# Front end of a hybrid decoder step: where the chunk row gathers, the second load of input weights and the first low weights are issued

## The reference, cut to what matters

```
xn = rms_norm(x, norm_attn_g)
z  = xn @ w_in                      # every q, k, v, gate and forget column at once
q, k heads = rms_norm per head
o_cmp, o_sel = nsa_cmp_sel(...)     # rows of cache_cmp_k/v in chunks of 16 -> small MLP -> compressed keys
                                    # and values, then attention on those and on the best 16 blocks
o_win = window_attend(...)          # last 512 rows
o_fox = fox_attend(...)             # logits plus sums of log forget gates, old ones from cache_fox_logf
h = x + (sig(ga) * (o_a @ w_o_a) + sig(gb) * (o_fox @ w_o_b)) @ w_out
y = h + (gelu(causal_conv3(rms_norm(h) @ w_up)) * (rms_norm(h) @ w_gate)) @ w_down
```

## Time and profile before

| | us |
|---|---|
| median of 3 runs | 945.47 |
| lowest and highest | 944.38, 947.38 |
| the profiled execution | 945.58 |
| its span, first to last instruction | 943.70 |

### The profile page before, as it was taken

How to read it: one execution, slowest core, us unless ns; L and a number is a source line. 1 busy time by engine, 2 the same in 40 slices (tenths; PEclk the granted TensorE clock), 3 DMA queues, 4 the chain that set the end, 5 groups by cost and what they waited for, 6 DMA issues and landing times. The chain is left out here.

```text
span 943.7 us, 18057 instructions
## 1 busy us (share of the span) xinstructions
PE 866.1 (92%) x7225; PEld 710.1 (75%) x7225; DVE 524.4 (56%) x980; ACT 367.8 (39%) x662; POOL 162.3 (17%) x262
## 2 busy tenths in 40 slices
PE   2999858989999999999999977999979999999996
PEld 1778747878988987665765455998669998989884
DVE  4556648743343567763466534565756565566554
ACT  3246445543334324453224321443344443534330
POOL 0200122210031012323334521000002010110100
PEclk9999969999999899999999989999989999999999
DMA  6434296039234339989999995986044544564412
GB/s 215 135 125 147 86 242 227 3 105 217 91 130 167 152 122 405 337 309 391 408 420 418 395 400 187 293 234 235 9 152 163 177 134 133 181 199 153 133 44 59
DMA packets 90608, 191.89 MB, mean 203 GB/s; under 512 B 7434, under 2 KB 68650, under 8 KB 78154
## 3 DMA queue, kind: packets, MB, share of 16 engines
q0 software_dynamic: 15408, 106.04, 29.3%
q1 hardware_dynamic: 73836, 84.43, 28.9%
q10 hardware_dynamic: 1296, 0.45, 0.2%
HBM read 187.44 MB, written 7.64 MB: 207 GB/s over the span
## 5 line engine op out<-in xcount | busy, mean ns | idle before, releaser
L1581 PEld LDWEIGHTS banks<-consts_base,stream_rows 128*128 128x128 f32 x672 | 73.2, 141 | 31.0 <-issue 27.3
L1828 ACT ACTIVATE keys_turned<-banks 128x512 f32<-128x512 f32 x94 | 55.0, 597 | 100.3 <-PE banks L1581 100.2
L258 PE MATMUL banks<-tokens_turned_high,w_gates_high 128*128 128x288 f32 x288 | 86.1, 299 | 3.5 <-PEq L191 2.3
L1581 PE MATMUL banks<-consts_base,stream_rows 128*128 128x128 f32 x672 | 82.5, 275 | 4.7 <-PEq L191 1.7
L259 PE MATMUL banks<-tokens_turned_low,w_gates_high 128*128 128x288 f32 x288 | 85.0, 295 | 0.0
L1120 PE MATMUL banks<-chunks_turned_high,cmp_w_high 64*128 64x256 f32 (+1 forms) x512 | 78.4, 300 | 5.3 <-DVE cmp_w_low L251 2.7
L260 PE MATMUL banks<-tokens_turned_high,w_gates_low 128*128 128x288 f32 x272 | 81.3, 299 | 0.0
L1120 PE MATMUL banks<-chunks_turned_low,cmp_w_high 64*128 64x256 f32 (+1 forms) x512 | 75.4, 288 | 0.0
L1120 PE MATMUL banks<-chunks_turned_high,cmp_w_low 64*128 64x256 f32 (+1 forms) x512 | 75.2, 287 | 0.0
L1809 DVE COPY keys_turned<-banks 128x512 f32<-128x512 f32 x74 | 50.4, 689 | 29.6 <-PE banks L1581 27.1
L251 DVE TENSOR_TENSOR chunks_turned_low<-banks,chunks_turned_high 128x512 fp32r<-128x512 f32 x64 | 41.1, 683 | 41.6 <-ACT chunks_turned_high L246 41.6
(11 more groups left out here) (446 smaller groups left out, 2114.6 us busy)
## 6 DMA issues: line engine op xcount, KB each, us to landing
w_up_gate<-in_w_up SPq DMA_DIRECT2D x12, 1024.0 KB, 7.4
w_up_gate<-in_w_gate SPq DMA_DIRECT2D x12, 1024.0 KB, 9.8
w_down<-in_w_down SPq DMA_DIRECT2D x12, 1024.0 KB, 5.1
w_in_slot<-in_w_in SPq DMA_DIRECT2D x8, 1424.0 KB, 6.2
w_gates<-in_w_in SPq DMA_DIRECT2D x10, 512.0 KB, 6.6
cmp_w<-in_cmp_w_k SPq DMA_DIRECT2D x4, 512.0 KB, 8.5
cmp_w<-in_cmp_w_v SPq DMA_DIRECT2D x4, 512.0 KB, 12.3
stream_rows<-in_state_win_k SPq DMA_DIRECT2D x8, 256.0 KB, 8.5
```

The lines of the kernel that those rows point to most:

```text
L258: nc.tensor.matmul(out, lh, rh, start=start, stop=False, **kw)
L1581: ins = nc.tensor.transpose(bank(t)[:, q * P:(q + 1) * P], src, ident)
L1828: copy = lambda a, b: nc.scalar.activation(a, b, ACT.Copy)
```

## The change

Three edits, all before the compression stage:

1. The four chunk row gathers leave POOL's list in `stage_project`, with POOL's three waits in front of them. In `stage_prompt` they stand behind POOL's copies; the m-th waits for `qk` to reach m + 1. The eight gathers of log forget values follow, and the b-th now waits for `qk` to reach b + 5.
2. The load of the second part of `w_in` leaves `stage_tokens` and becomes SP's first instruction in `stage_project`.
3. The low part of round 0 is made in two halves of four row groups each. The first half raises the new semaphore `first_low`, the second raises `low`. PE's wait before `tokens(0, 0)` is for `first_low`; a wait for `low` stands in the middle of it, before its fifth row group.

```diff
@@ stage_tokens, block.sync
-            for u in range(2):
-                load_w_in(c, sp, w, w_loaded, u, ORDER[u] * ZC)
+            load_w_in(c, sp, w, w_loaded, 0, ORDER[0] * ZC)
@@ stage_project
-        low = c.sem("w_in_low_ready")
+        low, first_low = c.sem("w_in_low_ready"), c.sem("w_in_first_low_ready")
@@ stage_project, block.sync
         def _(sp):
+            load_w_in(c, sp, w, w_loaded, 1, at(1))
             for n, g in enumerate(("k_norm_sel_g", "k_norm_win_g", "k_norm_b_g")):
@@ stage_project, block.gpsimd
             ins.then_inc(chunks.w2z, 1)
-            pool.wait_ge(low, NZC)
-            pool.wait_ge(z_sums, 3 * NZC - 2)
-            pool.wait_ge(heads_turned, number["QA", 2])
-            for m in range(NB):
-                chunks.gather(m)
@@ stage_project, block.tensor, tokens(n, t)
                 for k in range(KD):
+                    if (n, t, k) == (0, 0, KD // 2):
+                        pe.wait_ge(low, 1)
...
-                pe.wait_ge(low, n + 1)
+                if n == 0:
+                    pe.wait_ge(first_low, 1)
+                else:
+                    pe.wait_ge(low, n + 1)
                 tokens(n, 0)
@@ stage_project, block.vector
-            split(0)
+            dve.wait_ge(high, 1)
+            for half in range(2):
+                k = slice(half * KD // 2, (half + 1) * KD // 2)
+                split_low(nc, wl[0][:, k, :], w[0][:, k, :], wh[0][:, k, :]).then_inc((first_low, low)[half], 1)
@@ stage_prompt, block.gpsimd
             nc.gpsimd.tensor_copy(c.png[:, :, :], z[:, 0:2, O_NG:O_NG + 3 * NH])
+            for m in range(NB):
+                pool.wait_ge(qk, m + 1)
+                chunks.gather(m)
             link = c.chain(pool, "gpsimd")
             for b in range(DB):
-                pool.wait_ge(qk, b + 1)
+                pool.wait_ge(qk, NB + b + 1)
                 nc.gpsimd.indirect_dma_start(past_logf[:, b]...
```

## The result

The changed kernel takes 933.07 us (median of 6 runs, 930.44 to 936.61) against 945.77 us for the kernel before (6 runs, 944.38 to 947.66). The ratio is 0.987, with a 95% interval from 0.9851 to 0.9889. So the prediction was wrong in size: it expected a gain of 8.4 us and 12.7 came. The times of the changed kernel fall into two groups, 930.4 to 930.8 and 935.4 to 936.6, and its profiled execution is the slowest of the upper one: 936.61, with a span of 933.8 (2.8 lie around it, 1.88 before).

The account below looks back on a forecast made before the run. PE was taken as the bound inside project, with a gather-held hole before prompt. Gains of 7.6 + 0.5 + 0.3 = 8.4 us gave 937.1 us, range 933.5 to 940.5.

Parts of the forecast that it names:

- The hole, part 1: End of project: gathers in flight keep PE idle 10.5 us before prompt; moving them leaves about 2.9, gaining 7.6 us.
- The rival that it isn't the gathers': End of project: slow meeting or another transfer makes the hole; only 0.5 us gained, 945.0; 4 in 100.
- The cost of the moved gathers: Prompt stage: four gathers added on POOL delay log rows and sums, but within their cover; cost nothing.
- the bound of 163.6: Prompt stage: latest landing of the log rows, in us; the stage's end is delayed only if they land after 172.5.
- The clock in prompt: Early prompt: a shorter hole may keep PE at full clock; gain 0 to 2.0 us, taken as 0.3.
- the lower bound: Early prompt: no clock gain, 0 us, since PE still has a 2.9 us gap and the clock may fall there.
- Part 2's gain: Tokens stage: the second weight load came wholly after the first and took nothing from it; gain 0, at most 3 us.
- The rival with an earlier first slot: Start of project: first weight slot lands earlier, by up to 3 us, 1.5 in the middle; 935.6 us; 10 in 100.
- Part 2's cost: Project stage: moved load lands at 29.1 to 29.8, third weight part about 35.2, both in time; cost nothing.
- Part 3: Start of project: halving the first low part removes PE's 0.58 us wait; gain 0.34 to 0.58 us, taken as 0.5.
- The later stages: After the edits: a sign; the prediction is wrong if later stages lose what was gained; no size given.
- Part 2's own upper bound of 3: Tokens stage: at most 3 us gained if DMA engines that finish early slow the others through memory.

Follow-up runs that it names:

- e5: Kernel before with two of the four chunk gathers left in the project stage and two moved to prompt; 943.05 us (one run) beside 945.51.
- e6: Kernel before with the four chunk gathers replaced by four plain 1 MB loads of SP behind the same waits; 935.08 us (one run) beside 945.51.
- e2: Kernel before with only the second weight slot's load moved into the project stage; 944.01 us (12 runs), ratio 0.9975.
- e7: Kernel before with the page numbers loaded by SP in the project stage instead of by ACT in tokens; project started at 19.68 us, total time not given.
- e8: Changed kernel with the page numbers loaded by SP in the project stage, behind the gains; 943.5 us (12 runs), ratio 0.998 to the kernel before.
- e10: The changed kernel run again, nothing altered; 935.48 us (6 runs), ratio 0.9879 to the kernel before; its profiled execution is of the lower group.
- e14: Kernel before with only the first low part made in halves, a repeat profile; it and another repeat took 941.25 and 941.33 us.

## Why the prediction was right and where it failed

- **The hole, part 1: right, mechanism and size.** Forecast 7.60 (ends 7.36 and 7.60), measured 7.68 over three profiles of each. The stage's end stood 0.84 behind DVE, the forecast had 0.77 to 0.81. e5 gave the dose, e6 told POOL's gathers from SP's loads. The rival that it isn't the gathers' is out.
- **The cost of the moved gathers: right, nothing.** The log rows landed at 160.3, within the bound of 163.6, and the sums ended at 171.2 against 9.2 us of room. The last store was issued at 161.5.
- **The clock in prompt: no gain, forecast 0.3.** Prompt went from 66.06 to 66.45 in the means, within the scatter of single executions (65.76 to 66.66). The short hole is followed by the same half-clock stretch, 114.4 to 124.6, as the lower bound had it.
- **Part 2's gain: the step that failed, taken as 0, measured 2.4** (2.40 in the table, 2.15 and a median of 2.1 in e2). The argument was that the second slot came 3.76 us behind the first, its own transfer time, so it had taken nothing from it. That compares only two loads of SP's queue with each other. It left out what ACT's queue had in flight at the same time, the page numbers, although they landed only 8.1 to 12.9 us after issue in the kernel before. In the runs the second load cost the first 0.2 us without them, close to the argument's 0, and 2.2 with them. The prediction leant on the Trainium skill, page "DMA: Bandwidth & Descriptors", section "Queues, rings and completion order", for ring order; the page goes on that a later one may finish its write before an earlier one. That a later load doesn't delay an earlier one is the prediction's own conclusion and not the page's. The section also says that each DMA engine takes turns between the queues of different issuers. The runs agree with that (16.2 to 17.0 us from issue to landing with the page numbers on ACT's queue, 10.3 without, e7), but it doesn't say why the second load then costs 2.2. The rival with an earlier first slot was the true case, at 10 in 100 and with 1.5 in place of 2.4.
- **Part 2's cost: right, nothing.** The moved load landed at 26.80, ahead of the forecast 29.1, because project began earlier; its high part ended at 29.4 and PE never waited for it. The third part of the weights, issued at 25.90, was taken at 36.24, behind a wait of ACT's of 2.53, and PE didn't wait. How thin that cover is, e8 shows: with the page numbers in front of it PE stood for 8.4 us.
- **Part 3: the second step that failed, right in sign and mis-sized, 0.5 for 2.3.** The forecast gave two cases, that the clock rises at the same moment (0.34) or earlier by as much as the wait (0.58). It rose 4.2 us sooner after the start of the stage. The sentence "if it rises earlier by as much" was the place: the trace of before, at half clock from 22.94 to 30.7, had 7.8 us x 0.5 = 3.9 us at stake there, and the forecast bounded the gain by the wait and not by that.
- **The later stages: unchanged, within their scatter.** +0.54 from compress on in the means, with single executions 3.7 apart.

So 7.7 + 2.4 + 2.3 = 12.4, less 0.9 in the last two stretches, is the 11.4 between the mean spans; the medians differ by 12.7. The rest, 1.3, is no more than the share of executions with and without the late episode can move. That the measured 933.07 lies outside the stated range is part mechanism (the two steps above, 4.2 us in the stages) and part luck: over all 17 executions on record the median is 935.4.

Two ends that were known already would have widened the range. Part 2's own upper bound of 3 was put into a rival of 1.5, and the half clock at the start of project was not bounded at all.

## What to carry to other kernels

Don't let gathers of POOL be in flight when a stage that ends with a meeting of all engines ends; issue them just behind it. When a load is late, list what every issuer has under way at that time, small elements first: eight loads of 4 KB in all cost a load 4 to 7 us here, and another 1.4 MB behind it in its own queue 0.2 to 2.2. And before a small wait at the start of a busy stretch is priced, look whether the products behind it run at half clock: the most that can be won is then about half of that time, and not the wait.

## What the hardware showed that was not expected

- A meeting of all engines waits for POOL's own gathers to land (0.93 and 1.03 us from the last landing to the next stage, with two and four gathers), and not for SP's loads: in e6 one or more of four 1 MB loads were still in flight, and PE idled 2.90 us, as with none.
- Page numbers of 4 bytes each, 1024 of them, on ACT's queue held up a 1.4 MB load of SP's by some 6.3 us (16.2 to 17.0 us from issue to landing against 10.3) beside a second such load, and by some 4.3 without it (14.2 to 14.7 against 10.1).
- TensorE fell to 1.2 GHz for 6.8 us while it was busy for 6.80 of 6.80 us, in some executions and not in others; what it did before was a row of thin products (36 in 3.6 us, where it does 54 elsewhere). Such an episode costs 3.5 us, 0.4% of this kernel, which is more than part 2 brings.

```profile
298.40:302.00 3.60, 3.60 (x36) 3.51 (x33) 2.04 (x4) 1.09 (x2) 0.00 (x0) 1.00 0.10 39
```

This is the stretch of the profile after ahead of its episode (columns as above); e10 has the same 36 products there and no episode behind them. Why it comes in one and not in the other stays open.

- The column of the granted clock can read 1.00 where the products run at half clock. In e14 it does so from 18 to 26.4 us, though the sample products take 0.80 us and the next ones 0.50; in e10 it does so up to 23.4, though the sample products take 0.80. The duration of a product is the safer sign.
